# First attention of a two-block kernel: probabilities turned in 32x32 pieces and weighed a round later, with the feed-forward entry and the last block reordered

## The chip, the core and the metric

One core of a Trainium2 chip runs the whole program in one launch. The metric is the device time in microseconds (us); lower is better. All inputs and outputs are float32, the sequence is 512 tokens, the model is 1024 wide.

## What is computed

Two blocks follow each other. The first is a mixer (a gated causal convolution beside eight heads of attention) and a feed-forward part; the second is a hybrid layer (a state-space mixer beside attention over selected keys) and a final norm. The parts that the change touches:

```python
def first_block(...):
    h = rms_norm(x, g_mix)
    u, gb, gc, q, k, v = split(h @ w_in)
    y_conv = gb * short_conv(gc * u, conv_w)
    q = rms_norm(q, g_q) * HEAD_DIM ** -0.5      # per head of 64
    k = rms_norm(k, g_k)
    y_attn = dilated_mixture(q, k, v)            # causal; the dilated windows act as one mask of counts
    x = x + concat(rms_norm(y_conv, g_conv_out), rms_norm(y_attn, g_attn_out)) @ w_out
    h = rms_norm(x, g_ffn)
    x = x + (silu(h @ w_gate) * (h @ w_up)) @ w_down
...
def hybrid_layer(...):
    mod = silu(c) @ w_mod + b_mod                # shift, scale, gate
    h = rms_norm_2(x, norm_g) * (1 + scale) + shift
    ...
    return x + gate * (merged @ w_out)
...
out = rms_norm_2(x, final_g)
```

## The kernel before, in words

The program is written in raw form: five engine programs with semaphores between them, each executed in the order in which it is written. The banks of PSUM are PB[0] to PB[7]. Activations stand transposed (128 features on the partitions, 512 tokens along them): `xT` is the residual, `hH` and `hL` the high and low part of the normed input. Every large product is taken in three passes of float32r: high weights by high input, high by low, low by high. Its weights come as slots, numbered through the program: SyncE loads a slot (512 KB) into `raw`, ScalarE rounds it into `wH` (`split_hi`, L1051), VectorE subtracts and writes `wL` (`split_lo`, L1491), TensorE uses it in 24 matmuls (`project`, L573 to L575). There are two buffers of each, so a slot is split while the slot before it is used.

**The mixer** runs in four rounds (`mix`), each for one pair of heads and one quarter of the convolution. A round on TensorE: three projections (u, gc, gb), the turn of the values `vT` (L550), the scores of both heads against all keys up to each block of 128 queries (`split_scores`, L613 and L614, with q and k split in high and low copies `q1`, `k1`, `k1L` that ScalarE and VectorE make), the three projections of the next round's q, k and v, then `attend` (L626): 20 transposes of 128x128 of the probabilities `L` against the identity (L550), which ScalarE copies out of PSUM into `pT` (`p_evac`), and the weighing of the values with `pT` (L639). The sums of squares of the next q and k follow (`head_sums`, L690). On VectorE a round holds the norms, the convolution, mask and maximum of the scores (`score_max`, L1636), the scaling of the probabilities by the reciprocal of their sum (`normalise`, L1657 and L1661), six rows of the second block's modulation (`mod_rows`, L1670, whose weights `mraw` GpSimd loads two at a time), and six `split_lo`. The last round does not project a next q, k, v, but starts the output projection (`out_half`).

The weighing waits, for each block kb of keys, on the count `t_free` of ScalarE's copies:

```python
for kb in range(TB):
    pe.wait_ge(t_free, a * 8 + (kb + 9))
```

The same `attend` serves the four rounds of the second block's attention (`att`), where scores are taken in two-pass float32 on 64 rows (`scores`, L607) and their maxima by `head_max` (L1649).

**The feed-forward entry**: for each of eight output blocks d of the mixer's projection, VectorE adds into `xT` (L1771 to L1779), ScalarE and VectorE write the next `hH`, `hL` (L1221, L1758); the first two slots of the feed-forward part start on TensorE in an interleaved order (`project_two(first, each, late, ahead)`: all but the `late` last blocks of slot 0, then `ahead` blocks of slot 1, then the rest). **The down projection** (`down`, L817 to L819) takes 22 slots into eight banks. Its end feeds eight squares on ScalarE (L1265), of which VectorE adds the first `SQ_ADDED` = 4 (L1990) and TensorE sums the others (L833, L835). **The last block** (`last_half`, L1014 to L1016): the last two of eight output blocks of `w_out_2` are taken in halves of 256 tokens, added to `xT` (L2223), squared and scaled by ScalarE (L1446, L1447), transposed to tokens (`half_tokens`, L550), summed (`half_sums`, L1030), scaled by the root (L2254, L1463) and stored in four transfers of 512 KB (SyncE, L411).

Of the kernel before, what the change touches and what calls it, by code (L numbers as in the profile page):

```python
# [23 lines left out]
P = 128  # L24
S = 512
# [47 lines left out]
SQ_ADDED = 4  # L73
# [3 lines left out]
OFF = [0, 512, 896, 1152, 1280]  # L77

# [8 lines left out]
C_ID, C_DG, C_BD, C_M1, C_END = 0, 128, 256, 384, 896  # L87


def constants():  # L90
    i = np.arange(P)[:, None]
    d = i - np.arange(S)[None, :] + (S - P)
    c = ((d >= 0) & (d <= 128)) * 1 + ((d >= 0) & (d % 4 == 0)) + ((d >= 0) & (d % 16 == 0))
    m1 = np.where(c > 0, np.log(np.maximum(c, 1)), NEG)
    j = np.arange(P)[None, :]
    dg = np.where(j <= i, 0.0, 1.0)
    bd = (i // HD == j // HD) * 1.0
    return np.concatenate([np.eye(P), dg, bd, m1], 1).astype(np.float32)
# [30 lines left out]
def program(nc, io):  # L129
# [3 lines left out]
    out = io[-1]  # L133
    e_dram = nc.dram_tensor("rotations", [KH, P, 2, S], F32, kind="Internal").ap()

    with ExitStack() as ctx:
# [10 lines left out]
        def sem(name):  # L147
# [6 lines left out]
        LB, FB = ((PB[0], PB[3]), (PB[1], PB[5])), (PB[4], PB[7])  # L154
# [21 lines left out]
        ident, diag, bdones = cst[:, C_ID:C_DG], cst[:, C_DG:C_BD], cst[:, C_BD:C_M1]  # L176
# [45 lines left out]
        mtr = at("mtr", [P, D], F32, B0)  # L222
        wxH, wxL = at("wxH", [P, 1024], F32R, A0 + 32768), at("wxL", [P, 1024], F32R, A0 + 36864)
# [3 lines left out]
        q1 = [at(f"q1{e}", [P, S], F32R, B0 + 26624 + 2048 * e) for e in range(2)]  # L227
        k1 = [at(f"k1{e}", [P, S], F32R, B0 + 30720 + 2048 * e) for e in range(2)]
        k1L = [at(f"k1L{e}", [P, S], F32R, B0 + 34816 + 2048 * e) for e in range(2)]
# [41 lines left out]
        q_hi, q_lo, qx_hi, kx_hi = (sem(n) for n in ("q_hi", "q_lo", "qx_hi", "kx_hi"))  # L271
# [6 lines left out]
        sg_rdy, a32_rdy, ah_rdy, a_done, dn_done = (sem(n) for n in ("sg_rdy", "a32_rdy", "ah_rdy", "a_done", "dn_done"))  # L278
        pw_rdy, e_out, wk_rdy, wk_mm = sem("pw_rdy"), sem("e_out"), sem("wk_rdy"), sem("wk_mm")
# [18 lines left out]
        oh_mm, x3h, xfh, xfh_tr, oth, grh, fs_mm, f_ln, f_rs = (  # L298
            sem(n) for n in ("oh_mm", "x3h", "xfh", "xfh_tr", "oth", "grh", "fs_mm", "f_ln", "f_rs"))
# [28 lines left out]

        def blk(t, k):
            return t[:, k * P:(k + 1) * P]  # L330
# [5 lines left out]
        def _(sp_):  # L336
            sp_.dma_start(cst[:], consts[:, 0:C_M1]).then_inc(cst_in, 16)
# [68 lines left out]
            with sp_.Fori(0, KD // 2) as i:  # L406
                for s in range(2):
                    load(Slot(N_O2, s, 2, i), cols(w_out_2, i * (2 * P) + s * P))
            for t in range(TB):
                sp_.wait_ge(fin[t], 2 if t == TB - 1 else 1)  # L410
# [5 lines left out]
        def _(pool):  # L416
# [11 lines left out]
            pool.dma_start(mask1[:], consts[:, C_M1:C_END]).then_inc(mask_in, 16)  # L428


            def mod_loads(i):
                for m in range(6):
                    pool.wait_ge(m_used, i * 6 + (m + 2))
                    pool.dma_start(mraw[m % 2][:], w_mod_2[0][bass.ds(i * (2 * P) + (m // 3) * P, P),  # L434
                                                             (m % 3) * D:(m % 3 + 1) * D]).then_inc(m_full[m % 2], 16)
            with pool.Fori(0, NPAIR - 1) as i:
                mod_loads(i)
# [104 lines left out]

        @block.tensor
        def _(pe):
# [71 lines left out]
            def split_scores(a):  # L616

                for hh in range(2):
                    for b in range(TB):
                        pe.wait_ge(sc_free, a * 8 + (4 * hh + b + 1))  # L620
                        split_score(SB[b], b, q1[hh], k1[hh], k1L[hh]).then_inc(sc_ready, 1)

# [3 lines left out]
            def attend(a, v, vcol):  # L626

                for hh in range(2):
                    pe.wait_ge(pn, a * 2 + (hh + 1))
                    for kb in range(TB):  # L630
                        pe.wait_ge(t_free, a * 8 + (4 * hh + kb + 1))
                        transposes(TBANK[kb], [L[:, hh, CB[b] + P * kb:CB[b] + P * kb + P] for b in range(kb, TB)]
                                   ).then_inc(tr_mm, 1)
                wait(pe, o_free, a + 1)
                for kb in range(TB):
                    pe.wait_ge(t_free, a * 8 + (kb + 9))
                    for hh in range(2):
# [3 lines left out]
                        if kb == TB - 1:  # L641
                            ins.then_inc(pv, 1)

# [49 lines left out]
            def mix(i, last):  # L693
                for j in range(3):
                    project(Slot(3, j, 6, i))
# [17 lines left out]
                attend(i, vtok, lambda hh: slice(HD * hh, HD * hh + HD))  # L713
                if not last:
# [39 lines left out]
            with pe.Fori(0, NPAIR - 1) as i:  # L754
                mix(i, False)
            mix(NPAIR - 1, True)


# [34 lines left out]
            project_two(N_FF, x1l, 1, 2, last_pairs)  # L793
# [7 lines left out]
            def down(i, first, last):  # L801
                for s in range(2):
# [9 lines left out]
                    for d in (range(KD) if not first or s else (2, 3, 4, 5, 6, 7, 0, 1)):  # L812
                        a, z = first and s == 0, last and s == 1
# [5 lines left out]
                        ins = mm(PB[d][:], blk(wL[s], d), rh, start=False, stop=z, skip_group_check=True)  # L819
                        if z and d < KD - 1:  # L820
                            ins.then_inc(dn_done, 1)
                    ins.then_inc(slot_used, 1)
            down(0, True, False)
            pe.wait_ge(a_done, KF)
            with pe.Fori(1, KF // 2 - 1) as i:
                down(i, False, False)
# [1473 lines left out]
```

## Time and profile before

| | |
|---|---|
| median of 3 runs | 1007.94 us (1007.17 to 1008.73) |
| the profiled execution's own time | 1008.97 us |
| its span, first to last instruction | 1007.4 us |
| TensorE busy | 98% of the span |
| VectorE, ScalarE, GpSimd busy | 68%, 44%, 15% |
| TensorE on the chain that ended last | 95% |
| mean granted TensorE clock | 0.994 of full |

The durations used below come from the profiled execution, whose span is 1.6 us shorter than its own time. A matmul's record overlaps the next one's, so what a matmul costs is the distance from its start to the next start.

### The profile page before, as it was taken

The numbers are of one execution on the slowest core, as the hardware profiler recorded it, in microseconds if no ns is written. First come the engines' busy times: TensorE is split into PE (matmuls) and PEld (weight loads), VectorE is DVE, ScalarE is ACT, GpSimd is POOL, SyncE is SP. The second block draws the span as 40 slices with busy tenths as digits, with TensorE's granted clock in tenths as the row PEclk, the third lists the DMA queues.
The fourth block names the chain that finished last, engine by engine and source line by source line (L and its number), as shares of the span: only waits on it lengthen the run. The fifth ranks groups of instructions, "written<-read, shape, count | busy, mean of one in ns | idle before, by whom it ended". The sixth has DMA issues, their size and how long they took to land.

```text
span 1007.4 us, 14453 instructions
## 1 busy us (share of the span) xinstructions
PE 987.2 (98%) x4734; PEld 802.0 (80%) x4734; DVE 680.3 (68%) x1210; ACT 439.3 (44%) x725; POOL 155.2 (15%) x270
## 2 busy tenths in 40 slices
PE   6999999999999999999999999999999999999996
PEld 6887787777888888888888886888888887767886
DVE  5786786797766656645526568498978764665655
ACT  4656667543333332332311236945552334553333
POOL 3000100110000000864000000835750000000000
PEclk8999999999999999999999999999999999999998
DMA  6245534252533233244232223332233332112322
GB/s 209 85 133 160 171 99 146 66 146 83 153 117 104 86 102 103 85 146 142 90 104 88 99 75 105 98 87 68 64 105 100 87 105 63 44 62 84 104 84 84
DMA packets 145168, 104.11 MB, mean 103 GB/s; under 512 B 4636, under 2 KB 136988, under 8 KB 145132
## 3 DMA queue, kind: packets, MB, share of 16 engines
q1 hardware_dynamic: 139792, 85.96, 28.6%
q0 software_dynamic: 5104, 17.64, 5.7%
q8 instruction: 19, 0.31, 0.1%
q14 instruction: 17, 0.14, 0.0%
q10 hardware_dynamic: 236, 0.06, 0.0%
HBM read 99.45 MB, written 4.19 MB: 103 GB/s over the span
## 4 chain that ended last, share of the span: by engine, by line
PE 95%; ACT 2%; DVE 1%; issue 1%; DMA 1%; SPq 0%; DVEq 0%; ACTq 0%
PE bank L573 19%; PE bank L575 19%; PE bank L574 19%; PE bank L819 4%; PE bank L818 4%; PE bank L817 4%; PE bank L550 3%; PE bank L557 2%; PE bank L558 2%; PE bank L559 2%; PE bank L639 2%; PE bank L726 1%; PE bank L728 1%; PE bank L727 1%; PE bank L613 1%
## 5 line engine op out<-in xcount | busy, mean ns | idle before, releaser
L573 PE MATMUL bank<-hH,wH 128*128 128x512 f32 x840 | 328.6, 391 | 0.0
L575 PE MATMUL bank<-hH,wL 128*128 128x512 f32 x840 | 326.9, 389 | 0.0
L574 PE MATMUL bank<-hL,wH 128*128 128x512 f32 x840 | 326.9, 389 | 0.0
L1051 ACT ACTIVATE wH<-raw 128x1024 fp32r<-128x1024 f32 x155 | 164.2, 1060 | 270.6 <-PE bank L575 134.9
L1491 DVE TENSOR_TENSOR wL<-raw,wH 128x1024 fp32r<-128x1024 f32 x155 | 196.5, 1268 | 125.5 <-ACT wH L1051 124.6
L573 PEld LDWEIGHTS bank<-hH,wH 128*128 128x128 f32 x840 | 157.7, 188 | 36.2 <-issue 2.4
L575 PEld LDWEIGHTS bank<-hH,wL 128*128 128x128 f32 x840 | 157.7, 188 | 33.0
L574 PEld LDWEIGHTS bank<-hL,wH 128*128 128x128 f32 x840 | 157.7, 188 | 32.2
L819 PE MATMUL bank<-aH,wL 128*128 (+1 forms) x176 | 68.5, 389 | 0.0
L817 PE MATMUL bank<-aH,wH 128*128 (+1 forms) x176 | 68.5, 389 | 0.0
L818 PE MATMUL bank<-aL,wH 128*128 (+1 forms) x176 | 68.5, 389 | 0.0
L1800 DVE TENSOR_TENSOR ut<-bank,r 128x512 f32<-128x512 f32 x22 | 15.2, 691 | 49.9 <-PE bank L575 49.9
L434 POOL DMA_DIRECT2D mraw<-in_w_mod_dram x24 | 12.7, 529 | 202.4 <-DVE macc L1670 202.0
L1142 ACT ACTIVATE L<-L,nmx 128x128 f32<-128x128 f32 (+1 forms) x64 | 35.1, 550 | 11.5 <-DVE nmx L1652 10.7
L817 PEld LDWEIGHTS bank<-aH,wH 128*128 128x128 f32 x176 | 33.0, 188 | 6.9
L818 PEld LDWEIGHTS bank<-aL,wH 128*128 128x128 f32 x176 | 33.0, 188 | 6.9
L819 PEld LDWEIGHTS bank<-aH,wL 128*128 128x128 f32 x176 | 33.0, 188 | 6.7
L1670 DVE SCALAR_TENSOR_TENSOR macc<-mraw,csil,macc 128x1024 f32<-128x1024 f32 x24 | 30.2, 1281 | 9.6 <-DMA mraw<-in_w_mod_dram 9.6
L1051 ACT ACTIVATE aH<-a 128x512 f32 (+1 forms) x22 | 13.9, 632 | 45.9 <-DVE a L1804 45.9
L489 POOL COPY yaF<-yg 32x128 f32<-32x128 f32 x64 | 33.0, 515 | 2.9
L1806 DVE TENSOR_TENSOR aL<-a,aH 128x512 fp32r<-128x512 f32 (+1 forms) x22 | 17.2, 782 | 18.3 <-ACT aH L1051 18.3
L483 POOL DMA_DIRECT2D ebuf<-rotations x4 | 2.2, 563 | 154.8 <-PE bank L819 132.0
(465 smaller groups left out, 1520.0 us busy)
## 6 DMA issues: line engine op xcount, KB each, us to landing
raw<-in_w_in_dram SPq DMA_DIRECT2D x61, 512.0 KB, 3.5
mraw<-in_w_mod_dram POOLq DMA_DIRECT2D x24, 512.0 KB, 4.6
raw<-in_w_gate_dram SPq DMA_DIRECT2D x22, 512.0 KB, 3.6
raw<-in_w_up_dram SPq DMA_DIRECT2D x22, 512.0 KB, 3.5
raw<-in_w_down_dram SPq DMA_DIRECT2D x22, 512.0 KB, 3.2
raw<-in_w_out_dram SPq DMA_DIRECT2D x16, 512.0 KB, 3.5
x_tok<-in_x_dram SPq DMA_DIRECT2D x4, 512.0 KB, 7.4
rotations<-eb POOLq DMA_DIRECT2D x4, 512.0 KB, 5.1
```

What stands on the lines that cost most here:

```text
L489: ins = g.tensor_copy(dst(a, b), src(a, b))
L550: ins = nc.tensor.transpose(dst[0:m, t * P:t * P + kk], src, idn[0:kk, 0:kk])
L573: mm(o, a, hH[:, k, :], start=(k == 0), stop=False)
L574: mm(o, a, hL[:, k, :], start=False, stop=False)
L575: ins = mm(o, b, hH[:, k, :], start=False, stop=(k == KD - 1))
L817: mm(PB[d][:], blk(wH[s], d), rh, start=a, stop=False, skip_group_check=True)
L818: mm(PB[d][:], blk(wH[s], d), rl, start=False, stop=False, skip_group_check=True)
L819: ins = mm(PB[d][:], blk(wL[s], d), rh, start=False, stop=z, skip_group_check=True)
L1051: return A(o, i_, ACT.Copy, scale=scale)
L1142: ins = A(l, l, ACT.Exp, bias=nmx[:, c:c + 1], accum_out=rs[:, c:c + 1])
L1491: TT(wL[s.par][:], raw[s.par][:], wH[s.par][:].bitcast(F32), SU).then_inc(lo_done, 1)
L1670: STT(o, mraw[m % 2][:], col(csil, i * 2 + m // 3), o, MU, AD).then_inc(m_used, 1)
```

## The change

The first three rounds of the first attention no longer transpose the probabilities on TensorE. VectorE turns them in 32x32 pieces into `turned` (2560 columns a round), GpSimd issues four DMAs that spread these over the partitions in SBUF (`pTd`, which lies where `L` lay), ScalarE lays them out as `pT` (`laid_out`), and TensorE weighs them in the next round, between its second and third projection. The keys come out in an order that ScalarE's copy of `vT` matches. The last round still uses `attend`; its values are turned by 16 products of 32 columns. The scores are taken as in the second attention; the high and low copies of q and k go. Wherever `attend` is left, its weighing waits once, for all eight copies. In the second attention the tanh goes ahead of a `split_hi`. At the feed-forward entry `ahead` is 3 and one `split_lo` moves back; the last two slots of the down projection are interleaved, five squares are added by VectorE. The last block is taken by tokens: for each 128 tokens 24 products of 256 columns, with the residual transposed ahead of time, and a norm and a store per 128 tokens. The constants are loaded in two pieces.

```diff
-SQ_ADDED = 4
+SQ_ADDED = 5
...
-            sp_.dma_start(cst[:], consts[:, 0:C_M1]).then_inc(cst_in, 16)
+            sp_.dma_start(ident, consts[:, C_ID:C_DG]).then_inc(cst_in, 16)
...
+            def turned_moves(a):
+
+                pool.wait_ge(turn_rdy, 2 * TB * (a + 1))
+                settled(pool)
+                for q in range(TB):
+                    pool.dma_start(pTd[:, q].rearrange("p b c -> p (b c)"),
+                                   turned[32 * q:32 * q + 32].rearrange("p j b c -> p j (b c)")).then_inc(turn_in, 16)
...
+            def weigh(a, v, vcol):
+
                 wait(pe, o_free, a + 1)
                 for kb in range(TB):
-                    pe.wait_ge(t_free, a * 8 + (kb + 9))
...
+                pe.wait_ge(t_free, n * 8 + 12)
+                weigh(a, v, vcol)
...
+            def mix(i, first, last):
+                project(Slot(3, 0, 6, i))
+                project(Slot(3, 1, 6, i))
+                if not first:
+                    pe.wait_ge(turn_used, i + 1)
+                    weigh(i - 1, vtok, pair_cols)
+                project(Slot(3, 2, 6, i))
                 freed(pe, Slot(2, 0, 6, i))
-                transposes(PB[3], [vT[:, blkc(b)] for b in range(TB)]).then_inc(vtr, 1)
+                if last:
+                    for b in range(TB):
+                        for j in range(TB):
+                            ins = mm(PB[3][32 * j:32 * j + 32, blkc(b)], vT[:, P * b + j:P * b + P:TB], ident,
+                                     start=True, stop=True, skip_group_check=True)
+                    ins.then_inc(vtr, 1)
...
-                pe.wait_ge(q_lo, i + 1)
-                split_scores(i)
+                pe.wait_ge(qn_rdy, i * 2 + 2)
+                scores(i, qn, kn)
...
-            project_two(N_FF, x1l, 1, 2, last_pairs)
+            project_two(N_FF, x1l, 1, 3, last_pairs)
...
+                pe.wait_ge(lo_done, N_DN + KF - 1)
+                for d in range(KD // 2):
+                    block(0, d)
+                pe.wait_ge(lo_done, N_DN + KF)
+                for d in range(KD // 2):
+                    block(1, d).then_inc(dn_done, 1)
+                    ins = block(0, KD // 2 + d)
...
+            def laid_out(a):
+
+                act.wait_ge(turn_in, 16 * TB * (a + 1))
+                for hh in range(2):
+                    for kb in range(TB):
+                        ins = copy(pT[:, hh, OFF[kb]:OFF[kb + 1]].rearrange("p (b i c) -> p b i c", i=TB, c=32),
+                                   pTd[:, :, place_of(hh, kb), :].rearrange("p i b c -> p b i c"))
+                ins.then_inc(turn_used, 1)
...
+                A(thg[:], PB[3][:], ACT.Tanh, bias=hbg[:, bass.ds(i, 1)], scale=0.5).then_inc(th_rdy, 1)
                 if not last:
                     act.wait_ge(glu_full, i * 16 + 32)
                 split_hi(s.next())
-                A(thg[:], PB[3][:], ACT.Tanh, bias=hbg[:, bass.ds(i, 1)], scale=0.5).then_inc(th_rdy, 1)
...
+            def turn(hh, qb):
+
+                v.transpose(turned[:, :, places(hh, qb), :].rearrange("p j b c -> p b j c"),
+                            L[:, hh, CB[qb]:CB[qb + 1]].rearrange("p (b j c) -> p b j c", j=TB, c=32)
+                            ).then_inc(turn_rdy, 1)
...
                 mark(TT(xT[:, d, :], xT[:, d, :], wo1[:], AD))
+                if d == KD - 1:
+                    split_lo(sl.next())
                 freed(dve, sl)
...
-                if 0 < d < KD - 1:
+                if 0 < d < KD - 2:
                     split_lo(Slot(N_WO, d + 1).next())
...
+            def token_residual(t):
+
+                dve.wait_ge(tk_mm, t + 1)
+                dve.wait_ge(rows_in, 32)
+                last = slice(D - QD, D)
+                mark(TT(tkp[:, t, :], OT[t][:, 0:QD], rows[:, 0:QD], MU))
+                need()
+                TT(tkx[:, t, :], tkp[:, t, :], out_tok[:, t, last], AD).then_inc(x3t, 1)
+                dve.wait_ge(x3t, t + 1)
+                mark(TT(out_tok[:, t, last], tkx[:, t, :], rows[:, QD:2 * QD], MU))
```

On TensorE, the weighing of the first round of the second attention, with its waits. Before:

```order
L639 MATMUL bank<-pT,vt_205 64x512 [waits t_free,o_free]
L639 MATMUL bank<-pT,vt_205 64x512
L639 MATMUL bank<-pT,vt_205 64x384 [waits t_free]
L639 MATMUL bank<-pT,vt_205 64x384
L639 MATMUL bank<-pT,vt_205 64x256 [waits t_free]
L639 MATMUL bank<-pT,vt_205 64x256
L639 MATMUL bank<-pT,vt_205 64x128 [waits t_free]
L639 MATMUL bank<-pT,vt_205 64x128
```

And now:

```order
L662 MATMUL bank<-pT,vt_205 64x512 [waits o_free,t_free]
L662 MATMUL bank<-pT,vt_205 64x512
L662 MATMUL bank<-pT,vt_205 64x384 x2
L662 MATMUL bank<-pT,vt_205 64x256 x2
L662 MATMUL bank<-pT,vt_205 64x128 x2
```

Four waits, each for one copy more, have become one wait for all of them, ahead of the first product.

On VectorE, the scaling of the probabilities in a round of the first attention (`turned` is the buffer of 32x32 pieces, `macc` a modulation row, `wL` a slot's low part). Before:

```order
L1670 SCALAR_TENSOR_TENSOR macc<-mraw_102,csil,macc 128x1024
L1657 RECIPROCAL rinv<-rs 128x4
L119 REGISTER_ALU
L1661 TENSOR_SCALAR L<-L,rinv 128x128
L1661 TENSOR_SCALAR L<-L,rinv 128x256
L1661 TENSOR_SCALAR L<-L,rinv 128x384
L1661 TENSOR_SCALAR L<-L,rinv 128x512
L1657 RECIPROCAL rinv<-rs 128x4
```

And now:

```order
L1765 SCALAR_TENSOR_TENSOR mixL<-yc,vec,mixH 128x512
L1706 RECIPROCAL rinv<-rs 128x4
L1710 TENSOR_SCALAR L<-L,rinv 128x128
L1710 TENSOR_SCALAR L<-L,rinv 128x256
L1710 TENSOR_SCALAR L<-L,rinv 128x384
L1710 TENSOR_SCALAR L<-L,rinv 128x512
L1699 STREAM_TRANSPOSE turned<-L 128x4x32
L1699 STREAM_TRANSPOSE turned<-L 128x2x4x32
L1699 STREAM_TRANSPOSE turned<-L 128x3x4x32
L1699 STREAM_TRANSPOSE turned<-L 128x4x4x32
L1706 RECIPROCAL rinv<-rs 128x4
```

The first two modulation rows have gone behind the probabilities, and four turns stand behind each head's scaling.

On ScalarE, a middle round from the copy of u on. Before:

```order
L1051 ACTIVATE u_s<-bank 128x512
L1054 ISA
L1051 ACTIVATE wH_58<-raw_56 128x1024
L1051 ACTIVATE k_164<-kn 64x512 x2
L1059 REGISTER_ALU
L1054 ISA
L1051 ACTIVATE wH_57<-raw_55 128x1024
```

And now:

```order
L1106 ACTIVATE wH_58<-raw_56 128x1024
L1210 REGISTER_ALU
L1106 ACTIVATE pT<-pTd 128x512
L1106 ACTIVATE pT<-pTd 128x384
L1106 ACTIVATE pT<-pTd 128x256
L1106 ACTIVATE pT<-pTd 128x128
L1106 ACTIVATE pT<-pTd 128x512
L1106 ACTIVATE pT<-pTd 128x384
L1106 ACTIVATE pT<-pTd 128x256
L1106 ACTIVATE pT<-pTd 128x128
L1114 REGISTER_ALU
L1109 ISA
```

The copies of k have gone; the eight copies of the laid-out probabilities stand between two weight splits.

## Rows read from the trace of the kernel before

**Rows 1.** The page's first part, and its chain that ended last, by engine.
```profile
PE 987.2 (98%) x4734; PEld 802.0 (80%) x4734; DVE 680.3 (68%) x1210; ACT 439.3 (44%) x725; POOL 155.2 (15%) x270
...
PE 95%; ACT 2%; DVE 1%; issue 1%; DMA 1%; SPq 0%; DVEq 0%; ACTq 0%
```

**Rows 2.** Windows from round to round: length, busy time of each engine, clock, DMA share.
```profile
83.11:125.33 42.22, 42.01 (x212) 33.21 (x208) 32.51 (x57) 26.55 (x54) 3.16 (x6) 1.00 0.51 151
```

**Rows 3.** Timeline of TensorE, end of a round: start, length, engine, operation, count.
```profile
119.27 1.25 PE L550 MATMUL bank<-cst,L 128*128 128x128 f32 x10
...
122.01 2.38 PE L639 MATMUL bank<-pT,vtok 128*64 128x512 f32 x16
...
125.33 0.50 PE L573 MATMUL bank<-hH,wH 128*128 128x512 f32 x1
125.67 0.40 PE L574 MATMUL bank<-hL,wH 128*128 128x512 f32 x1
```

**Rows 4.** Timeline of ScalarE, the same stretch.
```profile
119.96 2.82 ACT L1051 ACTIVATE pT<-bank 128x512 f32<-128x512 f32 x8
```

**Rows 5.** Timeline of TensorE: values, then scores, split form and two-pass form.
```profile
99.56 0.60 PE L550 MATMUL bank<-cst,vT 128*128 128x128 f32 x4
99.92 0.30 PE L613 MATMUL bank<-k,q 128*128 128x128 f32 x1
...
102.92 0.40 PE L573 MATMUL bank<-hH,wH 128*128 128x512 f32 x1
...
829.34 3.02 PE L607 MATMUL bank<-kn,qn 64*128 64x128 f32 x16
832.29 0.50 PE L573 MATMUL bank<-hH,wH 128*128 128x512 f32 x1
...
856.33 1.77 PE L607 MATMUL bank<-kn,qn 64*128 64x384 f32 x8
```

**Rows 6.** Groups of VectorE by shape: count, busy us, mean ns.
```profile
L1852 DVE STREAM_TRANSPOSE mtr<-macc 128x1024 f32<-128x1024 f32 x3 | 3.7, 1237 | 0.0
L1681 DVE TENSOR_TENSOR q<-qn,q 64x512 fp32r<-64x512 f32 x4 | 2.7, 685 | 6.8 <-ACT k L1051 6.8
```

**Rows 7.** The tile mraw: issue to landing.
```profile
DMA to landing us min/median/max: 3.6/4.6/7.1
```

**Rows 8.** Timeline of TensorE, products of 32 columns in the second block's set-up.
```profile
608.48 1.95 PE L842 MATMUL bank<-s5W,cTt 128*32 128x128 f32 x64
```

**Rows 9.** Timeline of VectorE, the last round of the first attention.
```profile
186.87 1.22 DVE L1491 TENSOR_TENSOR wL<-raw,wH 128x1024 fp32r<-128x1024 f32 x1
```

**Rows 10.** Timeline of ScalarE, the second attention's last round.
```profile
902.16 1.04 ACT L1051 ACTIVATE wH<-raw 128x1024 fp32r<-128x1024 f32 x1
903.11 0.67 ACT L1395 ACTIVATE thg<-bank,hbg 128x512 f32<-128x512 f32 x1
```

**Rows 11.** Timeline of TensorE, the feed-forward entry.
```profile
245.46 0.50 PE L587 MATMUL bank<-hH,wH 128*128 128x512 f32 x1 [0.27 <-DVE hL L1758]
...
248.40 0.50 PE L587 MATMUL bank<-hH,wH 128*128 128x512 f32 x1 [0.58 <-DVE hL L1758]
```

**Rows 12.** Timeline of TensorE and VectorE behind the down projection.
```profile
604.10 1.02 PE L833 MATMUL bank<-sq,ones 128*128 128x512 f32 x2
...
606.35 0.69 DVE L1990 TENSOR_TENSOR sg<-sg,ss 128x512 f32<-128x512 f32 x1
...
607.53 1.02 PE L835 MATMUL bank<-sg,ones 128*128 128x512 f32 x2
```

**Rows 13.** Timeline of the end, then DMA throughput in 40 slices of the window 1002 to 1008 us.
```profile
998.37 0.38 PE L550 MATMUL bank<-cst,t 128*128 128x128 f32 x2
...
1003.07 0.35 DVE L2256 TENSOR_SCALAR out_tok<-out_tok,sm 128x256 f32<-128x256 f32 x1
...
GB/s 437 437 437 437 410 437 410 82 0 0 0 0 0 273 437 437 437 382 410 437 437 410 410 410 382 437 382 437 410 437 28 0 0 0 0 0 0 0 0 0
```

**Rows 14.** DMA issues of the first 20 us: size and median us to landing.
```profile
cst<-in_constants_dram SPq DMA_DIRECT2D x1, 192.0 KB, 2.3
```

More of the change, by code:

```diff
@@ L712, in mix @@
                     mm(PB[3][:], ones[:], ssc[:], start=True, stop=True).then_inc(ssm, 1)
-                attend(i, vtok, lambda hh: slice(HD * hh, HD * hh + HD))
-                if not last:
+                if last:
+                    attend(i, 0, vtok, pair_cols)
+                else:
                     head_sums(i + 1, Slot(7, 0, 6, i))
@@ L799, in _, with down @@
                     project(Slot(N_FF, s, 2, i))
-            def down(i, first, last):
+            def down(i, first):
                 for s in range(2):
@@ L812, in down @@
                     for d in (range(KD) if not first or s else (2, 3, 4, 5, 6, 7, 0, 1)):
-                        a, z = first and s == 0, last and s == 1
+                        a = first and s == 0
                         if a and d == 0:
@@ L997, in _ @@
             project_two(N_O2, mg_done, 2, 2)
+            for s in range(2):
+                transposes((PB[4], PB[7])[s], [xT[:, KD - 2 + s, blkc(b)] for b in range(TB)]).then_inc(x2_tr, 1)
             with pe.Fori(0, KD // 2 - 2) as i:
@@ L1001, in _, with token_products @@
                 project(Slot(N_O2, 3, 2, i))
[L1003 to L1006 removed]
+            def token_products(t, s):
                 sl = Slot(N_O2, KD - 2 + s)
[L1009 to L1017 removed]
@@ new lines, in token_products @@
+                if s:
+                    ins.then_inc(tk_mm, 1)
+            token_products(0, 0)
+            token_products(1, 0)
+            to_tokens(KD // 2 - 2)
+            token_products(0, 1)
+            token_products(1, 1)
+            pe.wait_ge(x2_ev, 2)
+            pe.wait_ge(gr_rdy, 1)
+            for t in range(TB):
+                ins = mm(FB[:, t:t + 1], gr[:, blkc(t)], ones[:, 0:1], start=True, stop=True)
+            ins.then_inc(fs_mm, 1)
+            for t in (2, 3):
+                pe.wait_ge(gfree[t % 2], Slot(N_O2, KD - 4 + t).gf)
+                for s in range(2):
+                    token_products(t, s)
@@ L1169, in mix @@
                 split_hi(u.next())
-                key_high(1)
+                if not first:
+                    laid_out(i - 1)
                 used(gc)
                 split_hi(gc.next())
+                if not first:
+                    values_out(i - 1)
                 used(gb)
@@ L1662, in normalise @@
                     ins.then_inc(pn, 1)
+                    if turning is not None:
+                        if hh:
+                            turning()
+                        dve.wait_ge(pn, a * 2 + (hh + 1))
+                        for b in range(TB):
+                            turn(hh, b)
             def mod_rows(i, ms):
@@ L1696, in mix @@
                 mark(STT(cv[:], cuP[:, 0:S], col(vec, i + V_CONV), cv[:], MU, AD))
+                if not first:
+                    values_low(i - 1)
+                    mod_rows(i - 1, range(4, 6))
                 used(gb)
@@ L1712, in mix @@
                     dve.nop().then_inc(cv_split, 1)
-                if not last:
-                    mod_rows(i, range(0, 2))
-                normalise(i)
+                normalise(i, None if last else lambda: split_lo(Slot(3, 3, 6, i).next()))
                 if last:
```

385 lines of the change are left out of this document (175 added, 210 removed).

## The prediction

> **What bounds the kernel now.** The first line of the page and the chain of waits come first: TensorE is busy 98% of the span and is 95% of the chain, while VectorE, ScalarE and GpSimd are busy 68%, 44% and 15% [rows 1]. So a part counts by what it takes from TensorE's stream or puts into it, or by a wait of TensorE that it makes. Next the windows from round to round: a round of the first attention lasts 42.22 us, of which TensorE works 42.01 at the full clock, VectorE 32.51 and ScalarE 26.55 [rows 2]. There is room for new work on these two, if it isn't late. Then TensorE's timeline, read from start to next start, since records overlap.
>
> **The three rounds whose probabilities are turned elsewhere.** The 20 transposes run from 119.27 to 122.01 [rows 3], so 2.74 us; three rounds lose them: **-8.2**. The weighing stays on TensorE, but now stands between two projections. The first product after the narrower ones has a record of 0.50, the next one 0.40 [rows 3]: 0.1 for the entry. One entry more for each of three rounds is **+0.3**.
>
> What takes the transposes over must fit. VectorE's known turn of 1024 columns took 1237 ns [rows 6], so 2560 columns take about 3.1 us; the source here is strided, so somewhat more is possible. It also loses six subtractions of 685 ns [rows 6] for the low parts of q and k, 4.1 us. Its load falls from 32.5 by about 1 us. ScalarE's eight copies out of PSUM took 2.82 us [rows 4]; eight copies from SBUF of the same widths replace them at about that price, at another place of the round, and copies of q and k go. GpSimd only issues four DMAs. The moves carry 1.3 MB, and a load of 512 KB that GpSimd issued landed after 4.6 us, 7.1 at worst [rows 7]. By my placing of the new order on the round of before, the turns end some 11 us after the round's first product and ScalarE wants the pieces some 12.5 us later (after the copy of u of the next round). So I cost turn, moves and copies at nothing. Their cover is the two projections and the three of the next round; were it gone, each microsecond of lateness would be one of TensorE, three times.
>
> The Trainium skill says in VectorE: DVE Perf Modes, section Rules for kernel authors, that 128x128 transposes belong to TensorE and that VectorE turns blocks of 32x32 only; taken as a price it speaks against this change, because the DMAs and copies behind the turn are the rest of a 128x128 transpose. The trace shows that TensorE has no free time and VectorE a quarter; by the rule the rounds would be no shorter.
>
> **The scores in two-pass form.** The split form took 99.92 to 102.92, 3.00; the two-pass form 829.34 to 832.29, 2.95, and the product behind it pays the entry of 0.1 [rows 5]. So +0.05 a round, **+0.2** over four. A faster case is there: eight of the products, half of the blocks but the wider ones, took 1.77 [rows 5]; with the narrower half at a half of that the form costs 2.65, so the bound is -1.0 for four rounds with the entry.
>
> **The weighing that waits for all copies.** Where `attend` is left (the last round here, four rounds of the second attention) the weighing used to start with the first copies. It started at 122.01 and ran without a gap [rows 3], while the copies ended at 119.96 + 2.82 = 122.78 [rows 4]; with one wait for all it starts at about 122.8, 0.8 later. Nothing stands between the transposes and the weighing, so TensorE idles: 5 x 0.8 = **+4.0**. This is the largest cost. Its bounds are 0, if something else of the stream covered it (I see nothing), and 5 x 0.9.
>
> **The last round of the first attention.** The values are turned by 16 products of 32 columns. The nearest row is 32 such products (64 records, two to a product) in 1.95 us [rows 8], so 0.95 for 16, where four transposes took 99.56 to 99.92, 0.36 [rows 5]: **+0.6**. The negated maxima now come for both heads together, with a weight split of 1.22 us [rows 9] ahead of the second head's. The exponents of the first head and all behind start later by up to that, and in this round the softmax is followed closely by the transposes: between 0 and 1.3, I take **+0.65**, the middle, since nothing shows how much slack is left.
>
> **The tanh.** In the second attention's last round ScalarE ran a weight split from 902.16 and the tanh from 903.11 [rows 10], and the output projection's second input waited for the tanh's result. Ahead of the split it comes 0.95 earlier: **-0.95**, between that and 0.
>
> **The feed-forward entry.** TensorE waited 0.27 and 0.58 for the last two `hL` [rows 11]. One more block of slot 1 ahead of them and a weight split of VectorE moved back take both away: **-0.85**; bounds -1.2 (with the gaps of re-entry) and 0.
>
> **Behind the down projection.** Four sums of squares took TensorE 604.10 to 607.53, so 0.86 each. One fewer is needed; but VectorE's last addition ended at 607.04 and the last sum began at 607.53 [rows 12], so VectorE, with one addition more of 0.69, becomes the later one unless its additions start earlier, which the interleaved end of the projection lets them. I take **-0.7**, between 0 and -0.86.
>
> **The last block and the tail.** The products are as many columns as before. TensorE gets some eight transposes more, 0.36 for four [rows 5]: +0.7. After the last product, 998.37 to 1003.42 passed before the last scaling ended [rows 13]. The transposes and the two squares of that stretch go, three steps of VectorE on 256 columns come; I take -0.45. The last store then was 1 MB and took about 17 slices of 0.15, 2.5 us [rows 13]; now 512 KB are last: -1.2. Sum **-0.95**, bounds -2 and +0.5.
>
> **The start.** 192 KB of constants landed after 2.3 us ahead of x [rows 14]; a third of that goes first now: **-0.3**, at best -0.8, at worst 0.
>
> **Sum:** -8.2 + 0.3 + 0.2 + 4.0 + 0.6 + 0.65 - 0.95 - 0.85 - 0.7 - 0.95 - 0.3 = -6.2. On the profiled execution, span 1007.4 and own time 1008.97, that gives 1001.2 and 1002.8; that execution was 1.0 above the median of 1007.94, from which I forecast **1001.7**.
>
> **The rivals.**
> (a) **The single wait costs nothing**, because the copies keep pace or the wait ends as soon as the first did. For it: the last of the four old waits was for the last copy too. Against: the weighing began 0.8 ahead of the last copy's end. 1001.7 - 4.0 = 997.7. Chance 0.05.
> (b) **VectorE binds in the rounds.** Turns of strided source at twice the known rate add 3 us to a stream that must deliver each low part on time: two weight splits and the normed inputs of the convolution stand behind the turns. With 1.3 us of slack ahead of the next split (my placing), 3 us would make some 1.3 of wait in each of three rounds, less what later projections absorb: +3.8, so 1005.5. For it: the turns stand in a block of eight with the scaling. Against: VectorE sheds 4.1 us. Chance 0.12.
> (c) **Slower than before: the moves land late.** ScalarE's copies stand in its program ahead of a weight split, so late pieces hold back the next projection's weights as well. If the four moves run one after another at 4.6 us each [rows 7], they take 18.4, 5.9 beyond the 12.5 of cover; three rounds: +17.7, 1019.4. It decides from 12.5 us on, and the change would lose as a whole from 6.2 / 3 = 2.1 beyond that, 14.6. For it: the pieces are many and short, and the DMA engines are already busy 51% of a round [rows 2] with weights. Against: a single load of 512 KB took 4.6 with that traffic, and the four spread over all engines. Chance 0.05.
> The Trainium skill gives in DMA: Bandwidth & Descriptors, section Anatomy of one DMA, 2.0 us plus bytes by 436 GB/s for a DMA issued by GpSimd, by which the four together would take about 5 us, an estimate from that page; by that rule (c) falls. No row here shows moves inside SBUF.
> (d) Several small terms (tail, start, feed-forward) go the wrong way, still faster than before: 1003.5 or so, in the forecast's own spread. Something not seen costs over 6 us: 0.02.
>
> **How the numbers follow.** The forecast with its spread has 0.76, (a) 0.05, (b) 0.12, (c) 0.05, the unseen 0.02. The bounds of the unknown terms: down by 1.2 (scores), 1.0 (tail), 0.65 (softmax), up by 1.5 (tail), 0.65, 0.85 and 0.7; not all together. So the range runs from 998.2 to 1005.6, which takes in (b), leaves (a) and (c) out. A measurement of this kernel tells about 0.2% (2 us) from no change: below 1005.9 is faster. Faster 0.93, same 0.02, slower 0.05.
>
> **What would show it.** In the profile after: rounds of the first attention of about 39.8 us, no transposes in three of them, the weighing with no idle time ahead; ScalarE's eight copies of `pT` ending ahead of the weighing; a wait on ScalarE of about 0.8 us ahead of each of five weighings (the strongest single test); no wait of TensorE on `hL` at the feed-forward entry; a last store of 512 KB. Wrong would be: idle time of TensorE in the three rounds on low parts (b), ScalarE idle on the moves (c), or copies slower from SBUF than 2.8 us for eight.

## The result and the profile after

The changed kernel took **1016.02 us** (median of 4 runs, 1015.08 to 1017.42) where the kernel before took 1008.32 in the same comparison: ratio 1.008, 95% interval 1.0064 to 1.0096. It is slower, where 1001.7 was forecast. The profiled execution took 1015.08, its span 1013.1, against 1007.4 of before.

The page's first part and its chain, after:

```profile
PE 982.6 (97%) x4700; PEld 790.0 (78%) x4700; DVE 675.8 (67%) x1217; ACT 424.1 (42%) x705; POOL 165.3 (16%) x286
...
PE 88%; DMA 4%; ACT 4%; DVE 2%; issue 1%; SPq 0%; ACTq 0%; DVEq 0%
PE bank L610 18%; PE bank L612 18%; PE bank L611 18%; PE bank L869 4%; PE bank L868 4%; PE bank L867 4%; DMA raw<-in_w_in_dram 3%; PE bank L662 2%; PE bank L644 2%; ACT pT L1106 2%; PE bank L587 2%; PE bank L594 2%; PE bank L775 1%; PE bank L777 1%; PE bank L776 1%; PE bank L596 1%
```

TensorE is busy 4.6 us less than in [rows 1], and yet the span is longer. It makes up 88% of the chain instead of 95%; DMA has gone from 1% to 4% of it, 3% being a load of weights (`raw`), and ScalarE's copies of `pT` are 2%. The windows from the first scores of a round to those of the next (columns as in [rows 2]) say where:

```profile
54.78:98.10 43.32, 40.10 (x189) 30.23 (x188) 30.94 (x59) 22.91 (x48) 5.04 (x9) 1.00 0.55 152
98.10:142.62 44.52, 41.85 (x189) 30.70 (x188) 31.33 (x59) 22.90 (x48) 5.57 (x10) 0.96 0.60 171
142.62:187.73 45.11, 42.46 (x218) 31.09 (x217) 31.84 (x59) 23.51 (x48) 4.91 (x9) 0.96 0.58 169
```

A round was 42.2 and was to be 39.8; it is 43.3 to 45.1, and two of three have a granted clock below 1. The timelines of ScalarE and TensorE in the first of them:

```profile
81.18 0.60 ACT L1106 ACTIVATE u_s<-bank 128x512 f32<-128x512 f32 x1 [2.75 <-PE bank L612]
85.69 1.06 ACT L1106 ACTIVATE wH<-raw 128x1024 fp32r<-128x1024 f32 x1 [3.91 <-DMA raw<-in_w_in_dram]
86.65 2.97 ACT L1106 ACTIVATE pT<-pTd 128x512 f32<-128x512 f32 x8
...
89.68 1.08 PE L662 MATMUL bank<-pT,vtok 128*64 128x512 f32 x4 [3.17 <-ACT pT L1106]
```

ScalarE waits 3.91 for a weight load, not for the moved probabilities; the eight copies behind it are as quick as forecast (2.97) but late, and TensorE waits 3.17 ahead of the weighing. In the next two rounds it waits 2.60 and 2.59, and the clock falls to its lower level (1.2 GHz) just behind: the weighing then takes 4.00 instead of 2.30. Windows of those stretches:

```profile
132.50:136.50 4.00, 4.00 (x16) 1.54 (x17) 3.69 (x6) 0.90 (x1) 1.25 (x2) 0.57 0.94 274
...
177.02:181.02 4.00, 4.00 (x16) 1.54 (x17) 3.93 (x6) 0.90 (x1) 1.12 (x2) 0.57 0.93 289
```

The waits are 8.4 us together. Two stretches of 3.4 us at half clock cost half their length each, so 3.4 in all: 11.8. Why that load is late, the issues show. SyncE issued it at 73.1 (the tile `raw`, window of that one load); ahead of it in the DMA engines stood four moves and two loads of modulation weights, which GpSimd had issued from 69.7 to 72.5. First `raw`, then `pTd` of that round, then `mraw`:

```profile
L363 SPq DMA_DIRECT2D raw<-in_w_in_dram x1: 372/372/372, 73.1 to 73.1; - x1
...
DMA to landing us min/median/max: 12.5/12.5/12.5
```
```profile
DMA to landing us min/median/max: 5.0/6.8/9.7
```
```profile
DMA to landing us min/median/max: 11.3/11.6/12.0
```

The last move, issued at 71.3, landed 9.7 later, at 81.0, ahead of ScalarE's copy of u (81.18): in time, by 0.8 us of the moment at which the copies would want it. The weight load landed at 85.7, 12.5 after its issue. The loads of this stretch before had a median of 3.7 and a maximum of 5.5; the load of the same slot, issued at 76.0, took 5.3:

```profile
DMA to landing us min/median/max: 5.3/5.3/5.3
```

Ahead of that load too stood two loads of modulation weights, issued at 72.9 and 74.8. What is new ahead of it are the moves, and behind them the modulation weights come late as well. DMA packets, bytes in MB and share of the 16 engines, changed kernel, first from 71 to 77 us, then from 77 to 81 (q0 is GpSimd's queue, q1 SyncE's):

```profile
q0 software_dynamic: 229, 0.96, 85.0%
...
q0 software_dynamic: 283, 1.06, 83.3%
q1 hardware_dynamic: 388, 0.20, 16.5%
```

Up to 77 not one packet of SyncE's queue was moved, though its load had been issued at 73.1; from there to 81 GpSimd's queue moved five bytes for each of SyncE's, in packets of mostly 4 KB beside packets of 512 bytes. And the moves are slow: up to 77 the engines carried 162 GB/s, from 77 to 81 they carried 313.

The rest of the difference, from one point of the stream to the same in the other trace: start to the first scores -2.9 (57.69 to 54.78); three rounds +6.3; last round of the first attention +1.5; feed-forward entry -0.9; feed-forward and end of the down projection -0.3; set-up of the second block -0.1; second attention +2.1; from its end on +0.1. The rounded terms add up to +5.8; the spans differ by 5.7.

### The profile page after: what moved, and what is told of

The parts are those of the page before. It is cut to its first block, busy times and chain, and to the rows that moved or that the text cites. A ratio compares the mean times of both kernels' runs of the same rounds, so it can differ in the third digit from the quotient of the medians.

```text
span 1013.1 us, 14288 instructions
## 1 busy us (share of the span) xinstructions
PE 982.6 (97%) x4700; PEld 790.0 (78%) x4700; DVE 675.8 (67%) x1217; ACT 424.1 (42%) x705; POOL 165.3 (16%) x286
## 4 chain that ended last, share of the span: by engine, by line
PE 88%; DMA 4%; ACT 4%; DVE 2%; issue 1%; SPq 0%; ACTq 0%; DVEq 0%
PE bank L610 18%; PE bank L612 18%; PE bank L611 18%; PE bank L869 4%; PE bank L868 4%; PE bank L867 4%; DMA raw<-in_w_in_dram 3%; PE bank L662 2%; PE bank L644 2%; ACT pT L1106 2%; PE bank L587 2%; PE bank L594 2%; PE bank L775 1%; PE bank L777 1%; PE bank L776 1%; PE bank L596 1%
## 5 line engine op out<-in xcount | busy, mean ns | idle before, releaser
L867 PE MATMUL bank<-aH,wH 128*128 (+1 forms) x160 | 62.3, 389 | 0.0
L868 PE MATMUL bank<-aL,wH 128*128 (+1 forms) x160 | 62.3, 389 | 0.0
L869 PE MATMUL bank<-aH,wL 128*128 (+1 forms) x160 | 62.3, 389 | 0.0
L867 PEld LDWEIGHTS bank<-aH,wH 128*128 128x128 f32 x160 | 30.0, 188 | 6.3
L868 PEld LDWEIGHTS bank<-aL,wH 128*128 128x128 f32 x160 | 30.0, 188 | 6.3
L869 PEld LDWEIGHTS bank<-aH,wL 128*128 128x128 f32 x160 | 30.0, 188 | 6.1
```

Source lines behind the costliest of these rows:

```text
L867: mm(PB[d][:], blk(wH[s], d), rh, start=a, stop=False, skip_group_check=True)
L868: mm(PB[d][:], blk(wH[s], d), rl, start=False, stop=False, skip_group_check=True)
L869: ins = mm(PB[d][:], blk(wL[s], d), rh, start=False, stop=False, skip_group_check=True)
```

## Experiments

Each ran beside the kernel before on the same chip; medians of that are 1007.0 (the first four), 1007.5 (the next four) and 1007.8 (the last three).

**Layout first.** What stands behind the late load on ScalarE?

```diff
+                if not first:
+                    laid_out(i - 1)
                 split_hi(u.next())
-                if not first:
-                    laid_out(i - 1)
```

> The eight copies of the moved probabilities stand ahead of ScalarE's weight split, not behind it. Theory Q (the moves landed in time, at 80.95 in the first round; the weight load behind them in the DMA engines landed 12.5 us after its issue, and ScalarE's fixed order hands that lateness to the copies): the copies start at 81.8 instead of 86.7, the weighing's idle time of 3.17, 2.60 and 2.59 us goes, and with it the two stretches of 3.4 us at half clock, 1.7 us each. 8.4 + 3.4 = 11.8 us less than the changed kernel: about 1004. Rival M (the moves themselves are late, or the copies slow): the copies wait for the moves instead, under 2 us less: 1014 or more. Rival L (the late weights then stop the third projection in place of the weighing): half of the gain, about 1010.

Measured 1013.69, ratio 1.0066 (1.0049 to 1.0083). The copies start at 81.63 as soon as u is copied, so the moves are in time and rival M falls; no wait stands ahead of the weighing in these rounds, and the window from the first scores to the second is 40.06 long. In time, 2.3 us less than the changed kernel (1.4 by the two ratios), it is near rival M's price all the same. The waits are back ahead of the scores. Timeline of VectorE and TensorE:

```profile
87.18 1.23 DVE L1548 TENSOR_TENSOR wL<-raw,wH 128x1024 fp32r<-128x1024 f32 x1 [8.01 <-ACT wH L1106]
...
98.31 0.68 DVE L1755 TENSOR_TENSOR yc<-bank,cv 128x512 f32<-128x512 f32 x1
...
98.91 0.28 DVE L1692 CUSTOM_DVE_ANT_0 L<-bank,mask 128x128 f32<-128x128 f32 x1
...
99.25 2.12 PE L644 MATMUL bank<-kn,qn 64*128 64x384 f32 x6 [3.53 <-DVE mx L1692]
```

VectorE too has its split of the late weights ahead of modulation rows, convolution and maxima, so it stood 8.01 us, and then worked without a gap until the scores' banks were due. Three waits of 3.5, 2.7 and 1.6 stand ahead of the scores, and the clock still fell twice. Rival L had the direction (less than the whole gain), not the size and not the place: the maxima, not the third projection. So this order on ScalarE alone is no cure: the late load stops VectorE next. Whether a new order on both engines would be one was not tried.

**Modulation loads later.** Which part of the backlog counts?

```diff
                     if m == 2 and between is not None:
                         between()
+                        pool.wait_ge(lo_done, i * 6 + (N_MIX + 11))
```

> GpSimd issues the third and fourth load of modulation weights of a round only when VectorE has split one weight slot more, some 5 us later, behind a weight load of SyncE. Theory Q1 (the 1 MB of modulation weights in the backlog is what makes the weight load late): it lands some 4 us earlier, the weighing waits under 0.5 us, the clock does not fall: 8 to 11.8 us less, 1004 to 1008. Theory Q2 (the moves alone, 1.31 MB in 11 us, hold the engines long enough): the weight load still lands past 82, idle time falls by 1 us or less a round: 1012 or more.

Measured 1004.45, ratio 0.9973 (0.9963 to 0.9983): faster than before. The weight load and ScalarE's row:

```profile
DMA to landing us min/median/max: 9.6/9.6/9.6
```
```profile
82.62 1.06 ACT L1107 ACTIVATE wH<-raw 128x1024 fp32r<-128x1024 f32 x1 [0.97 <-DMA raw<-in_w_in_dram]
```

It lands 3 us earlier (9.6 instead of 12.5), still far above the 5.3 of the same slot before, because of the moves, but that is nearly enough: the waits ahead of the weighing are 0.24 and 0.10, some 0.8 and 0.7 stand ahead of the scores, the clock never falls, rounds are 40.4 to 41.3. Against the changed kernel, by the two ratios to before, that is 1.07%, 10.8 us. The time is Q1's; the landing, at 82.6, is what Q2 foretold. So 3 us of landing a round, in three rounds, took away 6.5 of the 8.4 us of waits, and with the waits both stretches at half clock.

**Four waits again.** The wait for all copies is taken back.

```diff
                 for kb in range(TB):
+                    if n is not None:
+                        pe.wait_ge(t_free, n * 8 + (kb + 9))
...
-                pe.wait_ge(t_free, n * 8 + 12)
-                weigh(a, v, vcol)
+                weigh(a, v, vcol, n)
```

> The weighing in the five places that keep the old way waits again block by block. Theory of the record: each wait of 0.86 to 0.94 us goes back to 0.1: 5 x 0.8 = 4.0 us less, about 1012. Rival (the products then wait for the copies one by one, or a weight load was covered by it): under 1 us less, 1015 or more.

Measured 1011.17, ratio 1.0045 (1.0028 to 1.0062): 0.35% under the changed kernel's, 3.5 us. The same place in the changed kernel and here:

```profile
855.82 1.08 PE L662 MATMUL bank<-pT,vt 128*64 128x512 f32 x4 [0.86 <-ACT pT L1106]
```
```profile
855.59 1.73 PE L664 MATMUL bank<-pT,vt 128*64 128x512 f32 x8
```

The profiled execution of this run lost more in the three rounds than that of the changed kernel: waits of 2.28, 2.80 and 3.61, and one of its two stretches at half clock was 6.8 us long instead of 3.4. The four waits are told better by the pair without such stretches, modulation loads later with them and without: 0.9933 against 0.9973 below, 0.40%, 4.0 us, as forecast.

**The start alone.**

```diff
-            sp_.dma_start(cst[:], consts[:, 0:C_M1]).then_inc(cst_in, 16)
+            sp_.dma_start(ident, consts[:, C_ID:C_DG]).then_inc(cst_in, 16)
...
+            pool.dma_start(diag, consts[:, C_DG:C_M1]).then_inc(diag_in, 16)
```

> The kernel before with nothing but the constants in two pieces. The first scores came 2.9 us earlier in the changed kernel, and its start had no stretch at half clock where the one before had 6.8 us from 12.1 on. Theory C (192 KB ahead of x make TensorE idle 2.0 us at 11.7, and the clock falls for it): the first scores at about 55, no such stretch, 2.5 to 3 us less than before: about 1005.4. Rival (the start of a run differs by chance, or other edits did it): -0.3, about 1008.

The run also leaves out 64 KB of constants that nothing reads, as the changed kernel does. Measured 1006.23, ratio 0.9992 (0.9983 to 1.0002): not told from no change, though its profiled span is 3.1 shorter. The profiled execution of before had this, the changed kernel's and this one's had not:

```profile
12.14:18.97 6.83, 5.96 (x28) 5.96 (x29) 5.52 (x14) 5.10 (x10) 1.64 (x3) 0.50 0.33 92
```

The spans of the kernel before in 19 runs went from 1004.6 to 1007.5, with mean clocks from 0.998 down to 0.994, those of this kernel only from 1003.9 to 1004.8 at 0.997 and 0.998. So theory C fits what the profiles show, and its price in the median is wrong: the spread of spans and clocks speaks for a stretch that only some runs of before have. That is argued: the stretch itself was seen in profiles of single runs only. It also says how the sum stood: it was made against a profile whose start was at half clock, which not every run's is.

**Moves by SyncE.**

```diff
+                    if j == 2 and not first:
+                        turned_moves(i - 1)
                     load(Slot(3, j, 6, i), cols(w_in, i * P + z))
...
-                mod_loads(i, lambda: turned_moves(i))
+                mod_loads(i)
```

> The same four moves, issued by SyncE between its loads of the second and third slot of a round instead of by GpSimd. Theory Q (what counts is the bytes that stand ahead of the weight load in the DMA engines, whichever queue they came by): the weight load of the third slot still lands 9 us or more after its issue, the waits of 2.6 to 3.2 us ahead of the weighing stay within 1 us, total within 3 us of the changed kernel. Rival S (GpSimd's queue is served ahead of SyncE's, so the queue decides): the moves share the engines, the weight load lands in 6 us or less, and the weighing's idle time falls to under 1 us: about 8 to 11 us less.

Measured 1003.76, ratio 0.997 (0.9957 to 0.9983). In time it is rival S; in mechanism it is between. The load, now issued at 74.4 behind the moves, took 8.8 to land:

```profile
DMA to landing us min/median/max: 8.8/8.8/8.8
```
```profile
83.25 1.06 ACT L1109 ACTIVATE wH<-raw 128x1024 fp32r<-128x1024 f32 x1 [1.10 <-DMA raw<-in_w_in_dram]
```

So the bytes still count (8.8, not 5.3), but the whole backlog of moves, modulation weights and weights was through at 84.8 instead of 87.2 (landing of the second weight load), and the waits ahead of the weighing shrank to 0.37, none and 0.77. The modulation loads were issued at 71.2 and 72.4, nearly as in the changed kernel (71.8 and 72.5), so this is not their doing. The queue has a share of its own: with the modulation loads out of the way, in two runs below, the last move landed 11.0 us after the first was issued by GpSimd and 9.2 after the first was issued by SyncE. Why that is so stays open.

**The rest alone.** The kernel before with all but the first attention's edits and the single wait.

```diff
-SQ_ADDED = 4
+SQ_ADDED = 5
...
-            project_two(N_FF, x1l, 1, 2, last_pairs)
+            project_two(N_FF, x1l, 1, 3, last_pairs)
...
+                A(thg[:], PB[3][:], ACT.Tanh, bias=hbg[:, bass.ds(i, 1)], scale=0.5).then_inc(th_rdy, 1)
```

> The kernel before with every part of the change but the first attention's and the single wait: constants in two pieces, tanh ahead, feed-forward entry, end of the down projection, last block by tokens. From the spans between the same points of the two traces: start -0.75 (as the run with the start alone), feed-forward entry -0.9, tanh -0.95, end of the down projection 0, last block +0.1: 1004.4 against 1007.0 of before. Rival (the last block pays and only the wait at 935.74 hid it): below 1003.5. If it comes out under the run with late modulation loads and four waits, the turning itself is worth nothing.

Measured 1003.12, ratio 0.9958 (0.9945 to 0.9972): 4.4 us less than before. That is on the rival's side (below 1003.5): in its trace the wait of 1.04 us that the changed kernel has at 935.74 is absent, and the parts are worth 1.8 us more than the 2.6 that their spans in the two profiles told.

**Both mendings.** Modulation loads later and four waits, the two diffs above together.

> The changed kernel with the modulation loads behind a weight load and the block-by-block waits back. If both effects are apart from each other: 1004.45 less 5 x 0.8 = 1000.4, a ratio to before of 0.9935. Rival (the single waits covered a weight load that is then late): 1002 or more.

Measured 1000.44, ratio 0.9933 (0.9919 to 0.9946): the two effects add as forecast. It is 2.7 us under the run with the rest alone, on the same chip: so much are the first attention's edits worth together (turning, two-pass scores, the last round), with waits of 0.6 and 0.7 still in its rounds.

**No gather.** The 4-byte pieces of the gate row.

```diff
-            pool.dma_start(g_dram.rearrange("a (k p) -> p (a k)", p=P), mod[:, 3 * KD - 2:3 * KD],
-                           allow_slow_non_contiguous=True).then_inc(g_out, 16)
...
-            pool.dma_start(rows[:, 0:QD], g_dram[0:1, :].partition_broadcast(P)).then_inc(rows_in, 16)
+            pool.dma_start(rows[:, 0:QD], final_g_2.rearrange("(a n) -> a n", a=1)[:, 0:QD].partition_broadcast(P)).then_inc(rows_in, 16)
```

> As the kernel with both mendings, and the DMA that collects the last 256 gates from 4-byte pieces is left out, with its way back: the row holds other numbers, so the last 256 columns of the output are not the gated ones. Theory G (its 4-byte pieces hold up the weight load issued at 921.5, which took 11.8 us to land, and TensorE waits 1.0 at 935.7): no wait there, 0.4 to 1.0 us less than with it. Rival (the two loads of a row to all partitions do it): no difference.

Measured 1000.17, ratio 0.993 (0.9915 to 0.9945). The weight load issued behind it, with the gather (both mendings) and without:

```profile
DMA to landing us min/median/max: 11.3/11.3/11.3
```
```profile
DMA to landing us min/median/max: 4.3/4.3/4.3
```

The wait behind it is gone as well (0.48 with the gather). In the nine other profiles with the gather this load took 10.3 to 11.8. That 256 pieces of 4 bytes hold up a load by 7 us is shown; that it costs time is not: 0.3 us is less than the runs tell apart, and the wait was 1.04, 0.48, 0.17 and 0.06 in profiles of kernels alike in this part.

**Three more.** SyncE's moves added to both mendings; in the last round the weight split behind all maxima; and all together.

```diff
-                if last:
-                    head_max(i, masks1, lambda: split_lo(gb.next()))
-                else:
-                    head_max(i, masks1)
-                    split_lo(gb.next())
+                head_max(i, masks1)
+                split_lo(gb.next())
```

> Both mendings (modulation loads behind a weight load, block-by-block waits) and the moves issued by SyncE as well. The waits that are left in the rounds with both mendings are 0.6 ahead of the scores and 0.7 ahead of the weighing. If the two ways to shorten the backlog add up, they go: 999 to 999.5. Rival (with the modulation loads away the queue no longer matters): 1000.4, the same.

> Both mendings, moves by GpSimd, and in the last round of the first attention the weight split comes behind the maxima of all scores, not between them. Theory P (the negated maxima of both heads wait for that split of 1.22 us, and TensorE idles 0.87 ahead of the transposes for it): that idle time goes to 0.1, 0.8 us less: 999.6. Rival (the output projection then waits for the split): no gain, 1000.4.

> All of these together: 998.3 if each adds up; 1000.4 if none of the last two counts.

Measured 999.02 (0.991, 0.9897 to 0.9923), 1000.38 (0.9931, 0.9919 to 0.9943) and **998.00** (0.9908, 0.9895 to 0.9921). In the first of them no wait is left in the rounds:

```profile
55.30:95.34 40.04, 39.99 (x190) 30.22 (x189) 31.07 (x59) 22.91 (x48) 2.63 (x5) 1.00 0.57 164
95.34:135.47 40.13, 40.07 (x189) 30.23 (x189) 31.51 (x59) 22.91 (x48) 3.16 (x6) 1.00 0.65 190
135.47:176.22 40.75, 40.69 (x218) 30.61 (x217) 31.85 (x59) 23.51 (x48) 2.71 (x5) 1.00 0.66 187
```

With it the two ways to shorten the backlog stand in all four combinations. The weight load of the first round landed, in us after its issue:

| moves issued by | modulation loads as in the changed kernel | modulation loads later |
|---|---|---|
| GpSimd | 12.5 | 9.6 (9.1 with four waits) |
| SyncE | 8.8 | 6.1 (with four waits) |

Each way takes away some 3 us (2.7 to 3.7), with the other or without it. Behind SyncE's moves the load itself is issued some 1.3 us later, so that way makes it land some 2 us earlier, the other 2.5 to 3.

The last round's split gains nothing by its move: its wait of 0.87 ahead of the transposes becomes one of 0.56 at the output projection, and the rest of it lies within the runs' spread.

```profile
183.51 0.47 PE L777 MATMUL bank<-mixH,wH 128*128 128x512 f32 x1 [0.56 <-DVE wL L1550]
```

The last of the three beats both kernels, by 0.9% the one before; that it is better than the first of the three (998.4 to 999.1 against 997.6 to 999.7) is not shown.

## Why the prediction was wrong

**The step that failed** is "So I cost turn, moves and copies at nothing. Their cover is the two projections and the three of the next round." The steps under it held: turns ended at 69.0, moves were in place at 81.0 and wanted at 81.8, eight copies took 2.97 for 2.82. What I did not do is follow the queue behind the moves. I asked when the moves would land and not what they would make late. 1.3 MB of moves, with 1 MB of modulation weights issued right behind them, stood ahead of a weight load that nothing in the change touches; it landed after 12.5 us instead of 5.3, and ScalarE's and VectorE's fixed orders handed that on to the weighing (waits of 3.17, 2.60 and 2.59) or, with the order changed, to the scores. Making the backlog shorter, by either way, leaves waits of 0.8 and less.

**Rival (c)** had the sign and the engine on which it shows, ScalarE, but not the mechanism: it let the moves land late (18.4 us for four; they took 11.3 from the first issue to the last landing), and its price was 17.7. The Trainium skill's formula for one DMA issued by GpSimd (DMA: Bandwidth & Descriptors, section Anatomy of one DMA) made an estimate of about 5 us for the four together. The trace does not agree: it has 11.3, with the tail of a weight load ahead of them. The measurement decides, and the conclusion that I hung on that rule, that (c) falls, took from a rival what it should have kept: late transfers.

**Rival (b)** did not happen: VectorE worked 31 to 32 us of a round, less than the 32.5 before, and its turns took 3.4 us for 2560 columns (1.69 and 1.68 a head) where 3.1 was the forecast. The rounds of the changed kernel are no shorter, but for another reason than the Trainium skill's rule on where 128x128 transposes belong (VectorE: DVE Perf Modes, section Rules for kernel authors), and without the late load the rule is not borne out here: in the run with both mendings and SyncE's moves they are 40.0 and 40.1 against 42.2.

**The clock** was in no term. A wait of 2.6 us of TensorE was followed by 3.4 us at the lower level in two of three rounds, adding 1.7 to each; the longest wait, 3.17 in the first round, was not. With waits under 1 us it never was in these rounds.

**Term by term**, forecast and measured from the traces:

- Three rounds with the values' turn of the last: -7.1, +6.3. With nothing waiting a round took 40.04 for 42.23, so -6.6 for three against -7.8: the values' four transposes, now alone, take 0.53 for 0.36, and the projections 33.2 for 32.8, where 0.1 was reckoned. The forecast's round of 39.8 is 39.6 by its own terms. The values' turn itself took 1.04 for 0.35, +0.7 against +0.6: right.
- Single waits: +4.0. The waits were 0.86, 0.86, 0.94, 0.94 and 0.86, and the two pairs of runs that differ in them give 3.5 and 4.0: right, and it stays the second cost.
- The last round's softmax: +0.65, a wait of 0.86 behind the first ten transposes: right. With the single wait the round from its scores on is +1.5, forecast +1.45.
- Tanh: -0.95, the wait behind it fell from 1.55 to 0.62: right.
- Feed-forward entry: -0.85, -0.9: right.
- Behind the down projection: -0.7, -0.3. The sums take 3.6 for 4.4 us, but they start 0.4 later than the stream before them would let them.
- Last block: -0.95, +0.1. From the start of the last product on 7.0 us pass for 9.2, more than forecast, and 2.2 are lost ahead of it, 1.04 of these by the wait at 935.74, behind the load that the gather holds up.
- The start: -0.3, and -2.9 in the profiles, -0.75 in the medians.

So the late load was not the only miss. With the modulation loads later the time is 1004.45, inside the forecast's range, but only 2.5 us less than before where 6.2 were forecast. By the run with the rest alone the parts outside the first attention are worth 4.4 us, where their terms add up to 3.75: near. The first attention's edits without the single wait had terms of 6.45 and are worth 2.7 with both mendings and 4.8 with SyncE's moves as well (0.9958 against 0.991, on two chips).

## What to carry to other kernels

A transfer that lands in time can still cost time: list what is issued behind it in the DMA engines, by any queue, and ask for each of those when it is due. Where engines run in fixed order, a late load stops whatever stands behind its first user, so look first for what makes the load late; moving one user of it only moved the wait here. And a wait of TensorE of 2 to 3 us can cost more than its length because of the clock: 2.6 became 4.3 twice here.

## What the runs showed of the hardware

- A load of SyncE (512 KB) issued behind 2.3 MB of GpSimd's waited for nearly all of it: 12.5 us, 9.6 with the 1.3 MB of moves alone ahead, 5.3 for the same slot before. For 4 us after its issue none of its packets was moved; then GpSimd's packets, mostly of 4 KB, and its own, of 512 bytes, shared the engines at 1.06 to 0.20 MB in 4 us.
- Four moves inside SBUF of 320 KB each took 11.3 us in all. While they ran the engines carried 162 GB/s (71 to 77 us), and 313 when modulation weights and weights took over (77 to 81).
- The same four moves issued by SyncE, with the modulation loads away, took 9.2 us from the first issue to the last landing, issued by GpSimd 11.0, and the load behind them landed after 6.1 us instead of 9.1.
- A DMA of 256 pieces of 4 bytes held up a weight load of SyncE from 4.3 to 11.3 us.
- Waits of TensorE of 2.60 and 2.59 us were followed by 3.4 us at the clock's lower level, one of 3.17 in the first round was not. With the copies ahead of the split, 3.53 and 2.68 were, 1.55 was not. In the run with four waits 2.28 was not, 2.80 was, and with 3.61 came 6.8 us at the lower level.
